# Moving the decode keys ahead of the attention, and the zero rows behind it, in a hybrid decoder step

## The chip, the core and the metric

The kernel runs as one program on one core of a Trainium2 chip. The metric is device microseconds (us) of one execution. The engines are named as in the profile: PE (TensorE), DVE (VectorE), ACT (ScalarE), POOL (GpSimd) and SP (SyncE), which here only issues DMAs. PEld is PE's loading of weights.

## The reference, cut to what matters

One layer is computed for 512 prompt tokens and for 8 sequences that each decode 4 tokens against a cache of 2048 rows.

```python
h = rmsnorm(x, norm1_g) * (1 + sc1) + sh1
z = h @ w_in                                  # columns q | k | v | u
att = dilated_attn_prompt(q, k, v, rel_bias)  # prompt: three dilated windows, 8 heads x 64
att = dilated_attn_decode(q, concat(past_k, k), concat(past_v, v), rel_bias)  # samples
ssm_y = s5_branch(u, h0, ...)                 # scan, GELU, per-group GLU
mixed = concat([rmsnorm(att), rmsnorm(ssm_y)])
x = x + g1 * (mixed @ w_out)
x = x + g2 * hier_moe(rmsnorm(x, norm2_g) * (1 + sc2) + sh2)
y = rmsnorm(x)
```

## The kernel before

The order of the work on each engine is written out by hand; engines meet through counting semaphores, and an engine that waits holds back all that follows on it. The stages that matter here follow each other on PE:

1. **Values' projection.** `z_two(8)` to `z_two(11)` project the values, one block of 128 columns each, with `v_t(c)` turning a block over into `vrow`, and the 16 pieces of the SSM branch's GLU (`glu_in(n)` on PE, `glu_gate(n)` on ACT, `glu_out(n)` on DVE) in between.
2. **Flips.** `flip(h)`, one per head, makes the relative bias tile of a head by a matmul with a flipped identity; ACT copies it out (`bias_out`). Four blocks of decode keys of group 0 (`dec_keys(0, q)`) stand between the flips. Then 16 transposes of the SSM output (semaphore `ssT`).
3. **Attention of the prompt.** 16 steps `st`, for four pairs of heads and four tiles of 128 queries each; a tile of index `qt` has `m = 128 (qt + 1)` keys. A step is a chain: `scores(st)` on PE, `row_max(st)` on DVE, the exponential on ACT (`softmax`), the inverse on DVE, the product on POOL, `probs_t(st)` on PE two steps later, copies on ACT and DVE, `pv(st)` on PE three steps later. After each fourth step ACT copies a pair out (`pair_out`), and the next pair's first `pv` waits for that.
4. **Decode attention.** It is done for two groups of four sequences. For a group: `dec_keys` in four blocks, `dec_softmax` (DVE) and `dec_exp` (ACT), `dec_probs_t` (8 transposes on PE), `dec_probs` (copies on ACT and DVE), `dec_values` in four blocks, `dec_out` (DVE). Before the change, group 0's softmax stands ahead of the attention, its `dec_probs_t` in step 1, group 1's keys in steps 2 to 5, group 0's values in steps 9 to 12, group 1's `dec_probs_t` in step 13 and its values in steps 14 to 17.
5. **Output projection** `wo(p, half)`, which starts when ACT has written the last pair's part of `mixT`, then routing and the mixture of experts, whose weights stream in.

The cache is loaded by SP in 16 **cache blocks** `kv(0)` to `kv(15)`, then the two halves of `w_out` as `kv(16)` and `kv(17)`. Blocks 0 to 3 are group 0's keys, 4 to 7 group 1's keys (1792 KB each), 8 to 11 group 0's values, 12 to 15 group 1's values (2048 KB each, but 1024 KB for 11 and 15). They share three slots of a ring; `kv(i)` for i from 7 waits until `kvu`, the count of blocks used by PE, is i - 2 (for i from 2 to 5, i - 1; block 6 waits for the last value projection). SP issues in order: one blocked issue holds the next ones back. Among the blocks SP also issues the load of `mod3P`, the modulation rows for the later stages:

```python
for i in range(1, N_KV + 2):
    kv(i)
    if i == 9:
        sp.wait_ge(s("glut"), 16)
        for b in range(2):
            sp.wait_ge(s_modst[b], 64)
        sp.dma_start(mod3P[...], mod_rows(3, 2)).then_inc(s("mod3"), 16)
```

`mod_rows` reads, for each of the 128 partitions, 24 pieces of 128 floats out of `mod_d`; 1536 KB in all. POOL clears and fills `glu2` (the GLU's block diagonal weights) and `qbd` (the decode queries, block diagonal), writes 10 tiles of zero rows to `y_d` (5120 KB), takes part in each attention step, and later stores the rows `h2` and gathers them. In the rows below, L2053 is `z_half`, L2170 `glu_in`, L2182 `flip`, L2195 and L2202 `dec_keys`, L2217 and L2224 `dec_values`, L2280 `scores`, L2303 `pv`, L1955 every transpose, L2364 `wo`, L819 every operation of ACT.

Of the kernel before, what the change touches and what calls it, by code (L numbers as in the profile page):

```python
# [19 lines left out]
P = 128  # L20
# [24 lines left out]
EXTRA = 10  # L45
# [157 lines left out]
KMZ, PADT, BPAD, GLUB, QBD = range(1, 6)  # L203
# [25 lines left out]
def _build(nc, I, O, ctx):  # L229
# [82 lines left out]
    dPT = at("dPT", [P, 8, P], TAB + 12288)  # L312
# [149 lines left out]
    def _(sp):  # L462
# [106 lines left out]
        for i in range(1, N_KV + 2):  # L569
            kv(i)  # L570
            if i == 9:
                sp.wait_ge(s("glut"), 16)
                for b in range(2):
                    sp.wait_ge(s_modst[b], 64)
                sp.dma_start(mod3P[:, :, :].rearrange("p v (c j n) -> p (v c) j n", c=2, j=4),
                             mod_rows(3, 2)).then_inc(s("mod3"), 16)
# [92 lines left out]
    def _(pool):  # L669
# [65 lines left out]
        turn_back(4)  # L735
        turn_back(5)
# [13 lines left out]
        pool.wait_ge(s("xp"), len(BATCH))  # L750
        o(pool.memset(glu2[:, :, :, :], 0.0))
# [8 lines left out]
        o(pool.memset(qbd[:, :, :, :], 0.0))  # L760
        pool.wait_ge(s("za"), 8)
        for h in range(HEADS):
            r = slice(64 * (h % 2), 64 * (h % 2) + 64)
            o(pool.tensor_copy(qbd[r, :, h // 2, TDEC * h:TDEC * (h + 1)],
                               qkT[r, h // 2, 0:NS].rearrange("p (n t) -> p n t", t=TDEC)))
        pool.sem_inc(s("pool_prep"), 1)
        pool.dma_start(y_d[NREG * P:NTILE * P, :], I["zero"].partition_broadcast(EXTRA * P)).then_inc(s("yzero"), 16)
# [7 lines left out]


# [38 lines left out]
    def _(act):  # L815
# [175 lines left out]

        z_two(8)
# [8 lines left out]
        for n in range(7, 10):  # L1001
            glu_gate(n)
        z_two(11)
        v_out(2)
        for n in range(10, 13):
            glu_gate(n)
        v_out(3)
        f(vrow[0:NS, QT, :], ps[0:NS, 5, :], ACT.Copy).then_inc(s("ve"), 1)
# [22 lines left out]

        def dec_exp(g):
            act.wait_ge(s("dSm"), g + 1)
            f(dP[:, :], dP[:, :], ACT.Exp, bias=dstat[:, 4:5], accum_out=dstat[:, 5:6]).then_inc(s("dP"), 1)

        def dec_probs(g):
            act.wait_ge(s("dPt"), g + 1)
            if g:
                act.wait_ge(s("dOp"), g)
            f(dPT[:, 4:7, :], ps[:, 6, 0:3 * P].rearrange("p (a b) -> p a b", a=3), ACT.Copy)  # L1040
            f(dPT[0:NS, 7, :], ps[0:NS, 6, 3 * P:4 * P], ACT.Copy).then_inc(s("dPTe"), 1)
# [34 lines left out]
        dec_exp(0)  # L1076
        for st in range(NST + 3):
            if 2 <= st < NST + 2:
                probs_first(st - 2)
            if st < NST:  # L1080
                softmax(st)
            if st >= 3 and (st - 3) % QT == QT - 1:
                pair_out((st - 3) // QT)
            if 2 <= st < 10:
                ssm_square(st - 2)
            if st == 1:
                dec_probs(0)
            if st == 6:
                dec_exp(1)
            if st == 13:  # L1090
                dec_probs(1)
# [181 lines left out]
    def _(dve):  # L1273
# [260 lines left out]
        for n in range(16):  # L1534
            glu_out(n)

# [24 lines left out]

        dec_softmax(0)
        for q in (1, 3):
            dve.wait_ge(s("ssT"), q + 1)
            ts_(mixT[:, 4 + q, 0:SEQ], ps[:, (2, 3, 4, 7)[q], :], gains[:, 8 + q:9 + q], None, ALU.mult).then_inc(s("ssTe"), 1)
# [42 lines left out]
        for st in range(NST + 3):  # L1608
            if 1 <= st <= NST:
                inverse(st - 1)  # L1610
            if 2 <= st < NST + 2:
                probs_second(st - 2)
            if st < NST:
                row_max(st)
            if st == 1:
                dec_probs(0)
            if st in (11, 15):
                add_squares((st - 7) // 4)
            if st == 6:
                dec_softmax(1)  # L1620
            if st == 13:
                dec_out(0)
                dec_probs(1)
# [323 lines left out]
    def _(pe):  # L1947
# [199 lines left out]
        def v_t(c):  # L2147
# [5 lines left out]
            if c < 4:  # L2153
# [3 lines left out]
                tr(ps[0:NS, 5, P * c:P * (c + 1)], vT[:, c % 2, 0:NS]).then_inc(s("v"), 1)  # L2157
# [16 lines left out]
        def flip(h):  # L2174
# [3 lines left out]
            if h == 1:  # L2178
                pe.wait_ge(s("ve"), NT)
# [4 lines left out]
        def dec_keys(g, q):  # L2184

            r = ring_wait(pe, ("kv", 4 * g + q))
            if q == 0:
                if g == 0:
                    pe.wait_ge(s("pool_prep"), QBD)
                    pe.wait_ge(s("ve"), NT)  # L2190
# [48 lines left out]
        for n in range(3):  # L2239
            glu_in(n)  # L2240
        z_two(9)
        v_t(0)
        for n in range(3, 7):
            glu_in(n)
        z_two(10)
        v_t(1)
        for n in range(7, 10):
            glu_in(n)
        z_two(11)
        v_t(2)  # L2250
        for n in range(10, 13):
            glu_in(n)
        v_t(3)
        for h in range(2):
            flip(h)
        for n in range(13, 16):
            glu_in(n)
        for h in range(2, HEADS):
            flip(h)
            if h % 2 == 0:  # L2260
                dec_keys(0, h // 2 - 1)
        dec_keys(0, 3)
# [52 lines left out]
        for st in range(NST + 3):  # L2315
# [8 lines left out]
            if st == 1:  # L2324
                dec_probs_t(0)
            if 2 <= st < 6:
                dec_keys(1, st - 2)
            if 9 <= st < 13:
                dec_values(0, st - 9)
            if st == 13:  # L2330
                dec_probs_t(1)
            if 14 <= st < 18:
                dec_values(1, st - 14)
# [343 lines left out]
```

## Time and profile before

| what | value |
|---|---|
| three runs | 829.48 us median (827.67, 829.48, 833.77) |
| profiled execution | 830.8 us, its span 828.6 us |
| mean granted PE clock | 0.906 of full speed |
| PE busy | 672.9 us, 81% of the span |
| DMA | 211.86 MB, mean 256 GB/s |
| values' projection | about 202 to 246 us of the span |
| flips, keys of group 0 | 246 to 271 us |
| attention | 271 to 354 us |
| output projection, routing | 354 to 478 us |
| experts and end | 478 to 829 us |

The stages are read off the timeline of PE. The span leaves 2.2 us of the execution's own time outside.

### The profile page before, as it was taken

The numbers are of one execution on the slowest core, as the hardware profiler recorded it, in microseconds if no ns is written. First come the engines' busy times: TensorE is split into PE (matmuls) and PEld (weight loads), VectorE is DVE, ScalarE is ACT, GpSimd is POOL, SyncE is SP. The second block draws the span as 40 slices with busy tenths as digits, with TensorE's granted clock in tenths as the row PEclk, the third lists the DMA queues.
The fourth block names the chain that finished last, engine by engine and source line by source line (L and its number), as shares of the span: only waits on it lengthen the run. The fifth ranks groups of instructions, "written<-read, shape, count | busy, mean of one in ns | idle before, by whom it ended". The sixth has DMA issues, their size and how long they took to land.

```text
span 828.6 us, 11931 instructions
## 1 busy us (share of the span) xinstructions
PE 672.9 (81%) x4846; PEld 391.4 (47%) x4846; DVE 289.5 (35%) x691; ACT 176.2 (21%) x362; POOL 126.4 (15%) x224
## 2 busy tenths in 40 slices
PE   4668999999998875999994289876899999979800
PEld 3568787888862441434554244323344444323300
DVE  4799747741110542416634611100010011100047
ACT  6010421222232563422111001100110101100033
POOL 2310007559100331200000100000000000000040
PEclk9789999999999987999985589989899999999955
DMA  8995166656858979884219268999998549999562
GB/s 293 379 271 195 57 244 219 206 182 189 206 112 317 365 171 306 335 311 157 78 36 323 94 203 300 339 391 409 396 363 298 209 130 389 396 399 400 215 240 108
DMA packets 93580, 211.86 MB, mean 256 GB/s; under 512 B 8700, under 2 KB 15372, under 8 KB 93237
## 3 DMA queue, kind: packets, MB, share of 16 engines
q1 hardware_dynamic: 82550, 182.48, 62.3%
q0 software_dynamic: 4976, 18.37, 7.6%
q10 hardware_dynamic: 6000, 10.25, 3.4%
q8 instruction: 39, 0.64, 0.3%
q14 instruction: 15, 0.12, 0.1%
HBM read 197.42 MB, written 18.91 MB: 261 GB/s over the span
## 4 chain that ended last, share of the span: by engine, by line
PE 64%; DMA 14%; SPq 9%; DVE 6%; ACT 3%; issue 2%; POOL 1%; ACTq 0%; POOLq 0%; DVEq 0%
PE ps L2458 15%; PE ps L2053 11%; PE ps L2498 9%; PE ps L2364 7%; SPq L644 6%; DMA whalf<-in_w_down 5%; PE ps L1955 4%; DMA ring<-in_cache_v 4%; PE ps L2023 3%; PE ps L1961 3%; SPq L503 2%; DMA ring<-in_ada_w 2%; PE ps L2195 2%; PE ps L2170 1%; DMA ada_half<-in_ada_w 1%
## 5 line engine op out<-in xcount | busy, mean ns | idle before, releaser
L2458 PE MATMUL ps<-whalf,xgT 128*128 128x512 f32 (+2 forms) x576 | 175.1, 624 | 15.7 <-DMA whalf<-in_w_up 11.4
L2458 PEld LDWEIGHTS ps<-whalf,xgT 128*128 128x128 f32 (+2 forms) x576 | 67.5, 159 | 115.6 <-issue 110.7
L2498 PE MATMUL ps<-whalf,aT 128*128 128x512 f32 (+2 forms) x288 | 87.6, 625 | 13.8 <-DMA whalf<-in_w_down 11.9
L2053 PE MATMUL ps<-hT,ring 128*128 128x272 f32 x384 | 91.4, 394 | 0.0
L2053 PEld LDWEIGHTS ps<-hT,ring 128*128 128x128 f32 x384 | 71.8, 190 | 15.2 <-issue 1.4
L2498 PEld LDWEIGHTS ps<-whalf,aT 128*128 128x128 f32 (+2 forms) x288 | 33.3, 159 | 61.1 <-issue 58.7
L2364 PE MATMUL ps<-ring,mixT 128*128 128x512 f32 x128 | 60.0, 627 | 1.9 <-ACT mixT L819 1.9
L789 POOL DMA_INDIRECT xg<-h_d,gidx x12 | 11.5, 954 | 244.1 <-PE ps L1955 210.8
L2023 PE MATMUL ps<-hT,ring 128*32 128x136 f32 x1024 | 36.4, 301 | 5.4 <-DVE hT L1355 4.0
L1842 DVE COPY ysb<-ps 128x512 f32<-128x512 f32 x12 | 8.3, 691 | 92.3 <-PE ps L2498 92.3
L2364 PEld LDWEIGHTS ps<-ring,mixT 128*128 128x128 f32 x128 | 25.2, 201 | 32.2 <-issue 30.0
L773 POOL TENSOR_TENSOR Sb<-Sb,stat 128x128 f32<-128x128 f32 (+3 forms) x32 | 22.3, 719 | 113.1 <-DVE stat L1593 113.1
L1829 DVE SCALAR_TENSOR_TENSOR a_s<-a_t,ps 128x512 f32<-128x512 f32 x12 | 8.3, 688 | 89.6 <-ACT a_t L819 89.6
L1835 DVE SCALAR_TENSOR_TENSOR a_s<-a_s,ps 128x512 f32<-128x512 f32 x12 | 8.2, 687 | 88.7 <-PE ps L2458 88.7
L2023 PEld LDWEIGHTS ps<-hT,ring 128*32 128x32 f32 x1024 | 34.4, 119 | 6.3 <-ACT hT L819 4.2
L819 ACT ACTIVATE ysb<-ps 128x512 f32<-128x512 f32 x12 | 7.2, 597 | 106.0 <-PE ps L2498 106.0
L819 ACT ACTIVATE a_t<-ps 128x512 f32<-128x512 f32 x12 | 7.2, 597 | 101.2 <-PE ps L2458 101.2
L819 ACT ACTIVATE xgT<-ps 128x512 f32<-128x512 f32 x12 | 7.2, 596 | 83.8 <-PE ps L1955 83.8
L809 POOL DMA_INDIRECT yg<-y_d,sidx x10 | 10.1, 1015 | 96.2 <-DMA y_d<-ysb 93.5
L2217 PE MATMUL ps<-ring,dPT 128*32 128x512 f32 x112 | 15.4, 665 | 8.5 <-DMA ring<-in_cache_v 8.5
L819 ACT ACTIVATE Sb<-Sb,stat 128x128 f32<-128x128 f32 (+3 forms) x32 | 17.7, 553 | 20.1 <-DVE stat L1587 20.1
L1961 PE MATMUL ps<-ada_half,silu_c 128*32 128x128 f32 x512 | 18.3, 275 | 4.0 <-issue 2.3
(396 smaller groups left out, 913.2 us busy)
## 6 DMA issues: line engine op xcount, KB each, us to landing
whalf<-in_w_down SPq DMA_DIRECT2D x32, 1024.0 KB, 16.1
whalf<-in_w_gate SPq DMA_DIRECT2D x32, 1024.0 KB, 10.2
whalf<-in_w_up SPq DMA_DIRECT2D x32, 1024.0 KB, 14.7
ada_half<-in_ada_w SPq DMA_DIRECT2D x16, 1024.0 KB, 5.4
ring<-in_cache_k SPq DMA_DIRECT2D x8, 1792.0 KB, 7.4
ring<-in_cache_v SPq DMA_DIRECT2D x6, 2048.0 KB, 13.1
ring<-in_ada_w SPq DMA_DIRECT2D x4, 2048.0 KB, 14.6
ring<-in_w_in SPq DMA_DIRECT2D x4, 2048.0 KB, 13.2
```

The costliest lines, as they stand in the source:

```text
L503: sp.dma_start(cq[n][:, :, 0, :], I[name]).then_inc(s("ctl"), 16)
L644: sp.dma_start(half_dst(w, i), half_src(w, expert[m], half)).then_inc(efull[i], 16)
L773: tt(Sb[:, b, n, 0:m], Sb[:, b, n, 0:m], stat[:, 36 + 2 * b + n:37 + 2 * b + n].broadcast_to([P, m]), ALU.mult).then_inc(s("pn"), 1)
L819: return nc.scalar.activation(out, in_, func, **kw)
L1955: return mm(out, lhsT=in_, rhs=ident[0:n, 0:n], start=True, stop=True, is_transpose=True)
L1961: ins = mm(out[32 * j:32 * j + 32, 0:P], cS[:, k, :], r[:, 512 * (k - k0) + P * j:512 * (k - k0) + P * (j + 1)], start=k == 0, stop=k == K ...
L2023: ins = mm(ps[32 * j:32 * j + 32, b % 2, NCOL * i:NCOL * (i + 1)], r[:, 512 * k + c0:512 * k + c0 + 32], hT[:, k, j, :], start=k == 0, sto ...
L2053: ins = mm(ps[:, z % 2, 0:2 * NCOL], r[:, 512 * k + P * (c % 4):512 * k + P * (c % 4 + 1)], hT[:, k, 2 * h:2 * h + 2, :].rearrange("p a b ...
L2195: ins = mm(ps[32 * n4:32 * n4 + 32, 5 + part, 0:c1 - c0], qbd[:, 4 * g + n4, q, :], r[:, CK * n4 + c0:CK * n4 + c1], start=q == 0, stop=q ...
L2364: ins = mm(ps[:, 2 * half + n, :], mixT[:, k, tok(j)], r[:, 512 * k:512 * (k + 1)], start=k % 4 == 0, stop=k % 4 == 3)
L2458: ins = mm(out[cols, :], xgT[b][:, k, cols], r[:, 512 * (k % 4):512 * (k % 4 + 1)], start=k == 0, stop=k == KD - 1, **tile_at(m_, n))
L2498: ins = mm(ps[cols, 6 + n2, :], aT[:, t % 2, c, cols], r[:, c0:c0 + 512], start=c == 0, stop=c == 3, **tile_at(m_, n))
```

## The change

Group 0's keys go among the values' projection, with their softmax, exponential, transposes and copies; group 1's keys go among the last GLU pieces and the flips, with softmax and exponential ahead of the attention. In the attention remain group 1's transposes (step 1), group 0's values (steps 3 to 6), group 1's copies (step 7) and group 1's values (steps 8 to 11). `dPT` gets another place, the samples' part of `vrow` another PSUM bank (7 for 5). On POOL, `glu2` is cleared before the last `turn_back`, `qbd` is filled before `glu2`, and the zero rows are written after the attention's products. On SP, `mod3P` is issued after block 14 instead of block 9.

```diff
-KMZ, PADT, BPAD, GLUB, QBD = range(1, 6)
+KMZ, PADT, BPAD, QBD, GLUB = range(1, 6)
-    dPT = at("dPT", [P, 8, P], TAB + 12288)
+    dPT = at("dPT", [P, 8, P], CQR + 16384)
         for i in range(1, N_KV + 2):
             kv(i)
-            if i == 9:
+            if i == 14:
                 sp.wait_ge(s("glut"), 16)
...
         turn_back(4)
+        pool.wait_ge(s("xp"), len(BATCH))
+        o(pool.memset(glu2[:, :, :, :], 0.0))
         turn_back(5)
...
-        pool.wait_ge(s("xp"), len(BATCH))
-        o(pool.memset(glu2[:, :, :, :], 0.0))
+        o(pool.memset(qbd[:, :, :, :], 0.0))
+        pool.wait_ge(s("za"), 8)
+        for h in range(HEADS):
+            r = slice(64 * (h % 2), 64 * (h % 2) + 64)
+            o(pool.tensor_copy(qbd[r, :, h // 2, TDEC * h:TDEC * (h + 1)],
+                               qkT[r, h // 2, 0:NS].rearrange("p (n t) -> p n t", t=TDEC)))
+        pool.sem_inc(s("pool_prep"), 1)
         pool.wait_ge(s("glul"), 32)
...
         pool.sem_inc(s("pool_prep"), 1)
-        o(pool.memset(qbd[:, :, :, :], 0.0))
...
-        pool.dma_start(y_d[NREG * P:NTILE * P, :], I["zero"].partition_broadcast(EXTRA * P)).then_inc(s("yzero"), 16)
         for st in range(HEADS // 2 * QT):
...
+        pool.dma_start(y_d[NREG * P:NTILE * P, :], I["zero"].partition_broadcast(EXTRA * P)).then_inc(s("yzero"), 16)
 @@ ACT, values' projection @@
         for n in range(7, 10):
             glu_gate(n)
+        dec_exp(0)
         z_two(11)
         v_out(2)
+        dec_probs(0)
         for n in range(10, 13):
             glu_gate(n)
 @@ ACT, attention @@
-        dec_exp(0)
+        dec_exp(1)
         for st in range(NST + 3):
...
-            if st == 1:
-                dec_probs(0)
-            if st == 6:
-                dec_exp(1)
-            if st == 13:
+            if st == 7:
                 dec_probs(1)
 @@ DVE @@
+        for n in range(10):
+            glu_out(n)
         dec_softmax(0)
+        dec_probs(0)
+        for n in range(10, 16):
+            glu_out(n)
+        dec_softmax(1)
...
-            if st == 1:
-                dec_probs(0)
-            if st == 6:
-                dec_softmax(1)
-            if st == 13:
+            if st == 7:
                 dec_out(0)
                 dec_probs(1)
 @@ PE, flip and dec_keys @@
             if h == 0:
                 pe.wait_ge(s("toep"), 16 * HEADS)
-            if h == 1:
                 pe.wait_ge(s("ve"), NT)
...
                 if g == 0:
                     pe.wait_ge(s("pool_prep"), QBD)
-                    pe.wait_ge(s("ve"), NT)
+                    pe.wait_ge(s("buread"), 6)
@@ PE, order @@
         for n in range(3):
             glu_in(n)
+        dec_keys(0, 0)
         z_two(9)
         v_t(0)
         for n in range(3, 7):
             glu_in(n)
+        dec_keys(0, 1)
         z_two(10)
         v_t(1)
         for n in range(7, 10):
             glu_in(n)
+        dec_keys(0, 2)
+        dec_keys(0, 3)
         z_two(11)
         v_t(2)
+        dec_probs_t(0)
         for n in range(10, 13):
             glu_in(n)
         v_t(3)
+        dec_keys(1, 0)
         for h in range(2):
             flip(h)
         for n in range(13, 16):
             glu_in(n)
+        dec_keys(1, 1)
         for h in range(2, HEADS):
             flip(h)
-            if h % 2 == 0:
-                dec_keys(0, h // 2 - 1)
-        dec_keys(0, 3)
+            if h in (3, 5):
+                dec_keys(1, h // 2 + 1)
 @@ PE, attention @@
             if st == 1:
-                dec_probs_t(0)
-            if 2 <= st < 6:
-                dec_keys(1, st - 2)
-            if 9 <= st < 13:
-                dec_values(0, st - 9)
-            if st == 13:
                 dec_probs_t(1)
-            if 14 <= st < 18:
-                dec_values(1, st - 14)
+            if 3 <= st < 7:
+                dec_values(0, st - 3)
+            if 8 <= st < 12:
+                dec_values(1, st - 8)
```

## Rows read from the trace of the kernel before

**Rows 1.** Chain that ended last, 195 to 360 us: start, length, what.
```profile
290.07 33.72 DMA ring<-in_cache_v
```
**Rows 2.** Timeline of PE before the attention: start, us, line, tiles, form, count [idle before].
```profile
252.41 1.71 PE L2195 MATMUL ps<-ring,qbd 128*32 128x512 f32 x16
...
261.21 1.71 PE L2195 MATMUL ps<-ring,qbd 128*32 128x512 f32 x16 [1.63 <-DMA ring<-in_cache_k]
...
265.92 3.19 PE L2195 MATMUL ps<-ring,qbd 128*32 128x512 f32 x16 [1.95 <-DMA ring<-in_cache_k]
268.86 0.68 PE L2202 MATMUL ps<-qkT,qbd 128*32 128x32 f32 x32
269.47 1.96 PE L1955 MATMUL ps<-const,ssm_tok 128*128 128x128 f32 x16
271.37 0.49 PE L2280 MATMUL ps<-qkT 64*128 64x128 f32 x4
```
**Rows 3.** Timeline of PE in the attention.
```profile
291.63 0.92 PE L2280 MATMUL ps<-qkT 64*128 64x384 f32 x4
295.81 0.44 PE L2303 MATMUL ps<-PTs,vrow 128*64 128x128 f32 x4 [3.26 <-ACT attT L819]
...
296.76 2.08 PE L2280 MATMUL ps<-qkT 64*128 64x512 f32 x4
...
305.84 1.92 PE L2217 MATMUL ps<-ring,dPT 128*32 128x512 f32 x16
...
314.22 1.13 PE L2280 MATMUL ps<-qkT 64*128 64x512 f32 x4
323.84 3.64 PE L2217 MATMUL ps<-ring,dPT 128*32 128x512 f32 x16 [8.49 <-DMA ring<-in_cache_v]
...
328.80 0.49 PE L2280 MATMUL ps<-qkT 64*128 64x128 f32 x4
329.23 1.07 PE L2217 MATMUL ps<-ring,dPT 128*32 128x512 f32 x8
...
333.68 1.09 PE L1955 MATMUL ps<-const,dP 128*128 128x128 f32 x8
...
351.20 1.09 PE L2303 MATMUL ps<-PTs,vrow 128*64 128x128 f32 x16
354.22 8.83 PE L2364 MATMUL ps<-ring,mixT 128*128 128x512 f32 x16 [1.93 <-ACT mixT L819]
```
**Rows 4.** Timeline of SP's queue, issues around `mod3P`: start, us of the issue.
```profile
285.97 0.37 SPq L561 DMA_DIRECT2D ring<-in_cache_v  x1
286.46 0.43 SPq L575 DMA_DIRECT2D mod3P<-mod_d  x1
...
290.07 16.01 SPq L561 DMA_DIRECT2D ring<-in_cache_v  x1
```
**Rows 5.** Windows: busy times of engines, granted clock, DMA share, GB/s.
```profile
294.00:296.00 2.00, 0.19 (x4) 0.23 (x4) 1.48 (x7) 1.97 (x6) 0.34 (x1) 1.00 1.14 360
296.00:298.00 2.00, 2.00 (x12) 0.93 (x9) 0.42 (x1) 2.00 (x3) 1.27 (x2) 0.68 0.53 82
298.00:300.00 2.00, 0.92 (x4) 0.08 (x4) 1.11 (x3) 1.87 (x5) 0.00 (x0) 0.50 0.38 80
...
312.00:314.00 2.00, 0.73 (x7) 0.59 (x8) 0.17 (x1) 1.97 (x5) 1.08 (x2) 1.00 0.78 55
...
318.00:320.00 2.00, 0.00 (x0) 0.00 (x0) 0.17 (x1) 0.47 (x2) 1.19 (x2) 0.50 1.01 410
```
**Rows 6.** DMA issues, 180 to 480 us: count, KB each, median us to landing.
```profile
ring<-in_cache_k SPq DMA_DIRECT2D x7, 1792.0 KB, 7.4
...
y_d<-in_zero POOLq DMA_DIRECT2D x1, 5120.0 KB, 29.0
```
**Rows 7.** Timeline of POOL: the clearing of `glu2`, the last step's product.
```profile
195.09 3.53 POOL L751 MEMSET glu_blocks<- 128x4096 f32 x1
...
345.81 2.04 POOL L773 TENSOR_TENSOR Sb<-Sb,stat 128x512 f32<-128x512 f32 x2 [4.28 <-DVE stat L1593]
```

More of the change, by code:

```diff
@@ L759, in _ @@
         pool.sem_inc(s("pool_prep"), 1)
-        o(pool.memset(qbd[:, :, :, :], 0.0))
[L761 to L766, printed above, removed]
-        pool.dma_start(y_d[NREG * P:NTILE * P, :], I["zero"].partition_broadcast(EXTRA * P)).then_inc(s("yzero"), 16)
         for st in range(HEADS // 2 * QT):
@@ L990, in bias_out, with dec_exp, dec_probs @@
             f(biasT[:, h, :], ps[:, (7, 4)[h % 2], :], ACT.Copy).then_inc(s("bfe"), 1)
+        def dec_exp(g):
+            act.wait_ge(s("dSm"), g + 1)
+            f(dP[:, :], dP[:, :], ACT.Exp, bias=dstat[:, 4:5], accum_out=dstat[:, 5:6]).then_inc(s("dP"), 1)
+        def dec_probs(g):
+            act.wait_ge(s("dPt"), g + 1)
+            if g:
+                act.wait_ge(s("dOp"), g)
+            f(dPT[:, 4:7, :], ps[:, 6, 0:3 * P].rearrange("p (a b) -> p a b", a=3), ACT.Copy)
+            f(dPT[0:NS, 7, :], ps[0:NS, 6, 3 * P:4 * P], ACT.Copy).then_inc(s("dPTe"), 1)
         z_two(8)
@@ L1007, in _ @@
         v_out(3)
-        f(vrow[0:NS, QT, :], ps[0:NS, 5, :], ACT.Copy).then_inc(s("ve"), 1)
+        f(vrow[0:NS, QT, :], ps[0:NS, 7, :], ACT.Copy).then_inc(s("ve"), 1)
         bias_out(0)
@@ L1030, in _ @@
             f(mixT[:, 4 + q, 0:SEQ], ps[:, (2, 3, 4, 7)[q], :], ACT.Copy, scale=gains[:, 8 + q:9 + q]).then_inc(s("ssTe"), 1)
[L1032 to L1041, printed above, removed]
         NST = HEADS // 2 * QT
@@ L1532, in glu_out @@
                 op0=ALU.add, op1=ALU.mult).then_inc(s("glug"), 1)
-        for n in range(16):
-            glu_out(n)
         def dec_softmax(g):
@@ L2156, in v_t @@
                     ins = tr(ps[:, 4, P * t:P * (t + 1)], vT[:, c % 2, NS + P * t:NS + P * (t + 1)])
-                tr(ps[0:NS, 5, P * c:P * (c + 1)], vT[:, c % 2, 0:NS]).then_inc(s("v"), 1)
+                tr(ps[0:NS, 7, P * c:P * (c + 1)], vT[:, c % 2, 0:NS]).then_inc(s("v"), 1)
         def glu_in(n):
```

## The prediction

> **What bounds the kernel now.** I read the chain that ended last first, then the timeline of PE through the stages of the change, then SP's issues, then the DMA traffic in windows. The longest single piece of the chain between 195 and 360 us is a cache load of 33.72 us [rows 1]. Up to the attention PE is the bound: the values' projection, GLU pieces and flips run end to end, except that two key blocks wait for their loads, 1.63 and 1.95 us, and the second then runs at half speed, 3.19 us for a block that takes 1.71 otherwise [rows 2]. In the attention the bound changes from step to step between PE and the softmax chain, until PE stands 8.49 us before group 0's third value block and then runs it in 3.64 us instead of 1.92 [rows 3]. The block it waits for, cache block 10, was issued at 290.07, long before its use, so the question is what it waited behind. SP's queue shows it: block 9 at 285.97, `mod3P` at 286.46, block 10 at 290.07, whose issue alone took 16.01 us [rows 4]. The windows show why: the DMA engines move 360 to 410 GB/s until about 295.5, then 55 to 82 GB/s until about 315, then 410 again [rows 5]. 1536 KB at some 80 GB/s is 20 us, so that valley is `mod3P`, and block 10 went through the same queue behind it. From block 9's issue to block 10's landing at 323.8 it is 37.9 us.
>
> So what the change does to keys, softmax and values has to be weighed together with a line that its title doesn't name: `mod3P` moves from ahead of block 10 to ahead of block 15.
>
> **Part by part.** The values' projection and flips (one sum for PE, which is the bound there). Added: four key blocks of group 1 at 1.64 from start to start, 6.6 us; their new keys, 0.45; group 0's eight transposes, 1.0. Removed: the waits 1.63 and 1.95 and the 1.5 us of half speed, 5.1 us [rows 2]. The waits go because loads start earlier: block 0's use moves from 252.4 to about 212 (behind three GLU pieces), so block 2 is issued near 214 and used near 237, block 3 near 227 and 239, block 4 near 239 and 254, block 5 near 241 and 261, block 6 near 249 and 265, block 7 near 256 and 269. The least of these distances is 12 us, where a key block lands after 7.4 us [rows 6]. New on the path: ACT's two copies of group 0's probabilities stand ahead of GLU gate 10, about 0.6, and the last flip's copy on ACT, about 0.7, was hidden by the last key block and is not any more. The wait of `flip(0)` for all of `vrow` lies behind key block 4, which hides it; without that cover it costs 0.3. Sum 8.1 - 5.1 + 1.3 - 0.3 = **+3.9**, bounds +2.5 (neither of the new waits) and +5.2 (GLU pieces delayed twice as much). The first scores move from 271.4 to 275.3. DVE's and ACT's softmax of both groups lies beside projections and flips and costs nothing there; if PE were not the bound it would be about 3 us a group.
>
> POOL. Clearing `glu2` is 3.53 us [rows 7]; it goes into a wait of POOL ahead of the last `turn_back`, and as `qbd`'s part is pulled ahead of the copies into `glu2` by about as much, `glu2` is ready near 208, as before, where PE wants it at 209. I count 0; at worst 3.5 us of delay of the scan's last output, which PE would see.
>
> Attention, steps 0 to 11. Steps 2 to 5 lose key blocks and steps 3 to 6 get value blocks of 1.9 us [rows 3]; ACT and DVE lose group 1's exponential and softmax in step 6, and get both halves of the copies in step 7. Following scores, maximum, exponential, product, transposes and copies with the durations of the same steps before, the scores of step 6 come 1.2 us earlier against the first ones (three value blocks of 1.9 for four key blocks of 1.64), those of step 8 2.9 us (PE's wait for the first pair's copy is 1.3 instead of 3.26), and those of step 11 only 0.2 us, since step 8 held no decode work before and now has a value block, 1.9, and 1.3 of waiting for the copies. **-0.2**, bounds -2 and +1.
>
> The stall. Block 14 may be issued when group 0's last value block is used (`kvu` 12), in step 6, about 1.9 us after its scores. `mod3P` follows at once, and block 15, for which step 8 gives leave, stands behind it. Before, from scores 6 (291.63) to scores 11 (314.22) 22.6 us passed [rows 3]; with three value blocks in between instead of two and the copies of step 7 I take 23.5, so PE reaches group 1's last block 23.5 - 1.9 + 1.1 = 22.7 us after `kvu` 12. Block 15 lands later than that: the queue still holds part of block 13 and all of block 14, about 9.4 us at 400 GB/s, as much as it held ahead of `mod3P` before, so of the 37.9 us above only the half size of block 15 goes off, 2.6 us, and about 35.2 remain. PE stands 35.2 - 22.7 = 12.5 us, at 319 to 331.6, against 8.5 us before: **+4.0**. Bounds: with only block 14 ahead 10 us, with a slower end of `mod3P` 14 us. The loads of block 10, 11 and 12 to 14 are ahead of `mod3P` and each lands 5 us or more before its use. What runs right behind the stall is at half speed again, about 3.7 us, as before (3.64): 0.
>
> Steps after the stall. Between scores 12 (328.80) and the start of the output projection (354.22) three PE groups stood on the path: the end of group 0's values (2.0, from 329.23), group 1's transposes (1.0, from 333.68) and, at the end, values ahead of the last `pv` (351.20) [rows 3]. The last step's product on POOL ended at 347.85 [rows 7]; transposes and copy take 1.25 us from there, so that `pv` could have begun at 349.1, 2.1 us earlier. Of the 5.1 us I count **-4.7**, because the row maximum then ends last in step 12 and 13; bounds -3.5 and -5.1.
>
> PE's clock in the last steps. Before, PE idled 3.26 us for a pair's copy at 292.5 to 295.8 after a busy stretch, and the granted clock then fell to 0.68 and 0.50, scores of 512 taking 2.08 us instead of 1.13 [rows 3, 5]. After the change step 14 has no value block, and the chain there (maximum, exponential, copy of the pair) leaves PE idle for the same 3.26 us between scores 14 and `pv(12)`. Then scores 15 (+1.0), half of the last transposes (+0.4) and the last `pv` (+1.0) run at half speed: **+2.4**, or 0 if the clock holds. I take 2.4, as the row is the nearest one there is. The output projection began at half clock before too (8.83 us for a block of about 7.1), so nothing changes there.
>
> Zero rows. They are 5120 KB and took 29.0 us to land [rows 6]. Now they are issued near 354, beside the first expert halves, rows of x and the samples' modulation. The bound is the chain of PE, ACT and DVE there, and what it needs next from memory, the third tile's rows of x and the storing of the first tile's `h2` rows (which POOL issues behind the zero rows), is due near 410. All traffic due by then is about 50 us of the DMA engines from 351 on: 0, with some 10 us to spare. It is no gain either, since nothing waited for DMA when the zero rows were written before, except that it slows no cache load now.
>
> Sum: 3.9 - 0.2 + 4.0 - 4.7 + 2.4 = **+5.4 us**. The profiled execution took 830.8 us (span 828.6 and 2.2 around it), so it would take 836.2; the median of the runs is 1.3 us lower, and there the forecast is 829.48 + 5.4 = 834.9, rounded 835. All that follows, the experts' stream above all, starts later by the same and is not changed by it. With the bounds, most of them not at once, this case by itself lies between 829 and 839.
>
> The Trainium skill speaks against the stall: the page "DMA: Bandwidth & Descriptors", section "Specifications", gives 512 B as the smallest transfer at line rate, and pieces of 128 floats are just that. By its 358 GB/s `mod3P` would take an estimated 4.4 us, and block 15 would land ahead of its use. The trace disagrees: 55 to 82 GB/s while `mod3P` has the queue alone [rows 5]. I go by the row.
>
> **The rivals.** First, a clear queue: `mod3P` doesn't hold block 15 for as long as PE needs to reach it, because it is faster beside other traffic or because the blocks ahead are done sooner. Then scores 12 follow at about 322.4 instead of 328.8, 6.4 us earlier, and with the gain of 4.7 behind and the clock's 2.4 or 0 it is -8.7 to -11.1 us: 818 to 821. For it speaks that all blocks up to 14 are early; against it the same `mod3P` in [rows 4, 5], which held a block for 18 us with nothing else in the queue. 0.10. In between, a stall of 3 to 7 us gives 822 to 828: 0.08.
>
> Second, slower: the zero rows overrun. Its place is the third tile of the output projection: POOL's store of the first `h2` tile, if served in order behind the zero rows, lets ACT overwrite that buffer only near 402, and SP's rows of x for the third tile share the engines with the zero rows. It decides from the point where either lands after about 410; from there each us is paid in full. A write at half the rate (58 us for 29) would put it at 412 to 420, so +2 to +10 on top: 841 or so. Against it: the prefetches share evenly and none of them is due before 478. 0.08.
>
> Third, the change doesn't do what it says, since keys of group 0 wait for their loads in the projection as they did in the flips: 3.6 us more in that stage, but the stall behind it is counted from step 6 and comes later by the same. It would be 838 to 839; at 12 us distance I give it no chance of its own.
>
> **How the numbers follow.** Forecast 0.74 (829 to 839 and a little beyond), clear queue 0.10, short stall 0.08, zero rows 0.08. The range leaves out the clear queue and the far end of the zero rows and reaches a little beyond the forecast's own bounds: 824 to 842. A measurement of this kernel tells about 1%, 8.3 us, from no change: faster means below 821.2, slower above 837.8. The clear queue is faster, mostly; the zero rows and the upper end of the forecast, with a tenth of it, are slower: 0.09, 0.75, 0.16.
>
> **What would show it.** Right: no wait of PE for key blocks; first scores near 275; `mod3P` issued near 297 with a slow issue of block 15 behind it; a wait of PE of 10 to 14 us for cache values, now at the last block of group 1 and in step 11; some 21 to 23 us from scores 12 to the output projection, part of it at clock 0.5. Wrong: no such wait, with the output projection before 346; or a wait of ACT or DVE for rows of x or `h2` between 390 and 430; or a GLU piece that waits for POOL at 209.

## The result, and the profile after

The changed kernel takes 839.12 us (median of 4 runs, 836.52 to 842.36), the kernel before beside it 828.94 us (4 runs, 827.67 to 833.77). The ratio is 1.0097, 95% interval 1.0056 to 1.0137, which is 4.6 to 11.4 us more (the two medians alone stand at 1.0123, 10.2 us). The forecast was +5.4 us, 835.0. The profiled execution of after, the fastest of its four runs, took 836.5 us (span 834.2), that of before 830.8 (span 828.6): +5.7.

The stages in front of the change differ by a microsecond or more from one profiled execution to the next. So times in the attention are counted here from one event, the first product of the GLU. In the timeline of PE it stands, in the kernel before, at

```profile
209.03 3.09 PE L2170 MATMUL ps<-glu_blocks,u_chunks 128*128 128x256 f32 x12
```

and in the kernel after, with the rows that answer to [rows 2, 3]:

```profile
210.40 3.09 PE L2167 MATMUL ps<-glu_blocks,u_chunks 128*128 128x256 f32 x12
...
255.33 1.71 PE L2191 MATMUL ps<-ring,qbd 128*32 128x512 f32 x16
...
275.51 0.49 PE L2282 MATMUL ps<-qkT 64*128 64x128 f32 x4
...
305.94 3.49 PE L2213 MATMUL ps<-ring,dPT 128*32 128x512 f32 x16 [1.99 <-ACT dPT L819]
...
320.28 1.13 PE L2282 MATMUL ps<-qkT 64*128 64x512 f32 x4
331.07 1.94 PE L2213 MATMUL ps<-ring,dPT 128*32 128x512 f32 x8 [9.66 <-DMA ring<-in_cache_v]
...
337.32 0.80 PE L2282 MATMUL ps<-qkT 64*128 64x128 f32 x4
...
347.45 0.69 PE L2305 MATMUL ps<-PTs,vrow 128*64 128x128 f32 x4 [3.26 <-ACT attT L819]
...
349.12 2.08 PE L2282 MATMUL ps<-qkT 64*128 64x512 f32 x4
```

No key block has a wait any more. The first scores are at 275.51 (forecast 275.3). The one wait for a cache load has moved to group 1's last value block, behind scores 11, and ends at 331.07 (forecast 331.6). Both times are counted from the span's start and hold 1.4 us that this execution lost ahead of the first GLU product, outside the change. Later PE stands 3.26 us for a pair's copy, and then come scores of 512 at 2.08 us instead of 1.13. Three pieces of the chain that ended last (start, length, what) answer to [rows 1]:

```profile
309.47 21.55 DMA ring<-in_cache_v
...
331.07 1.94 PE ps L2213 x8
...
361.30 8.55 PE ps L2362 x16
```

SP's issues answer to [rows 4]. `mod3P` is issued at 296.80, as forecast (297). The slowest issue is not, as forecast, that of the cache block behind it (4.58 us) but that of `w_out` behind the block (12.35 us for its two halves):

```profile
296.80 0.48 SPq L575 DMA_DIRECT2D mod3P<-mod_d  x1
309.47 4.58 SPq L561 DMA_DIRECT2D ring<-in_cache_v  x1
314.10 12.35 SPq L554 DMA_DIRECT2D ring<-in_w_out  x2
```

The windows answer to [rows 5]; the last two columns are DMA share and GB/s, the one before them the granted clock:

```profile
298.00:300.00 2.00, 1.48 (x10) 1.09 (x12) 0.43 (x2) 1.97 (x3) 1.61 (x2) 0.83 1.00 393
...
312.00:314.00 2.00, 2.00 (x20) 0.56 (x22) 0.97 (x6) 0.96 (x4) 0.00 (x0) 1.00 0.56 86
...
322.00:324.00 2.00, 0.00 (x0) 0.00 (x0) 1.53 (x6) 0.99 (x3) 0.00 (x0) 0.81 0.63 59
328.00:330.00 2.00, 0.00 (x0) 0.00 (x0) 0.00 (x0) 0.00 (x0) 0.00 (x0) 0.50 1.05 409
348.00:350.00 2.00, 2.00 (x8) 1.22 (x8) 0.42 (x1) 1.84 (x3) 0.71 (x1) 0.50 0.05 12
```

The valley is the same as before, only later: 393 GB/s at 298 to 300, and so on up to 306, 52 to 92 in the windows from 308 to 326, while `mod3P` is under way, and 409 when the last block comes. Of the DMA issues, two answer to [rows 6]; nobody waited for either of them behind the attention:

```profile
y_d<-in_zero POOLq DMA_DIRECT2D x1, 5120.0 KB, 32.1
...
mod3P<-mod_d SPq DMA_DIRECT2D x1, 1536.0 KB, 31.5
```

From the first GLU product to four later events of the PE timelines (scores 0, 11, 12 and the output projection), in us, from one profiled execution of each kernel, and the times of all runs; each ratio is to the kernel before on the same chip:

| kernel | scores 0 | scores 11 | scores 12 | output proj. | median us | ratio, 95% interval |
|---|---|---|---|---|---|---|
| before | 62.3 | 105.2 | 119.8 | 145.2 | 828.94 | 1 |
| after | 65.1 | 109.9 | 126.9 | 150.9 | 839.12 | 1.0097 (1.0056 to 1.0137) |
| e1_mod3p_last | 65.2 | 109.9 | 114.3 | 137.5 | 829.16 | 0.9913 (0.9877 to 0.9949) |
| e2_old_order_mod3p_last | 60.6 | 103.5 | 107.8 | 133.2 | 822.09 | 0.9859 (0.9804 to 0.9913) |
| e3_mod3p_after_9 | 65.1 | 123.4 | 127.9 | 153.1 | 842.18 | 1.0112 (1.0080 to 1.0143) |
| e4_zero_rows_early | 74.1 | 116.2 | 137.5 | 161.4 | 849.15 | 1.0145 (1.0087 to 1.0203) |
| e5_values_late | 65.1 | 108.7 | 114.8 | 140.4 | 828.84 | 0.9932 (0.9898 to 0.9967) |
| e6_mod3p_on_act | 65.2 | 110.1 | 129.0 | 152.4 | 838.55 | 1.0090 (1.0057 to 1.0123) |
| e7_wide_pieces_probe | 65.1 | 108.7 | 113.2 | 136.4 | 820.65, one run | |
| e8_narrow_pieces_probe | 65.1 | 110.0 | 114.4 | 138.9 | 828.86, one run | |
| e9_old_order_two_keys_early | 59.0 | 101.8 | 106.1 | 131.6 | 821.15 | 0.9856 (0.9813 to 0.9898) |
| e10_new_order_mod3p_wide | 65.0 | 107.7 | 112.2 | 136.8 | 825.24 | 0.9898 (0.9851 to 0.9945) |
| e11_two_keys_early_mod3p_wide | 59.0 | 101.8 | 106.1 | 131.5 | 819.86 | 0.9832 (0.9791 to 0.9873) |
| e12_old_order_mod3p_wide | 61.0 | 103.9 | 108.2 | 133.7 | 822.94 | 0.9882 (0.9838 to 0.9926) |

The kernel before stood at 833.1 us (833.04 to 833.14) beside all the experiments, so their medians are read by the ratio and not against 828.94.

### The profile page after: what moved, and what is told of

It is laid out like the page before. It is cut to its first block, busy times and chain, and to the rows that moved or that the text cites. A ratio compares the mean times of both kernels' runs of the same rounds, so it can differ in the third digit from the quotient of the medians.

```text
span 834.2 us, 11931 instructions
## 1 busy us (share of the span) xinstructions
PE 673.4 (81%) x4846; PEld 390.1 (47%) x4846; DVE 289.7 (35%) x691; ACT 176.7 (21%) x362; POOL 126.5 (15%) x224
## 4 chain that ended last, share of the span: by engine, by line
PE 64%; DMA 12%; SPq 10%; DVE 7%; ACT 3%; issue 3%; POOL 1%; ACTq 0%; POOLq 0%; DVEq 0%
PE ps L2456 15%; PE ps L2050 11%; PE ps L2496 9%; PE ps L2362 7%; SPq L644 6%; DMA whalf<-in_w_down 5%; PE ps L1952 4%; PE ps L2020 3%; DMA ring<-in_cache_v 3%; PE ps L1958 2%; SPq L503 2%; DMA ring<-in_ada_w 2%; PE ps L2191 2%; PE ps L2167 1%; PE ps L2213 1%
## 5 line engine op out<-in xcount | busy, mean ns | idle before, releaser
L2362 PE MATMUL ps<-ring,mixT 128*128 128x512 f32 x128 | 57.8, 608 | 1.9 <-ACT mixT L819 1.9
L772 POOL TENSOR_TENSOR Sb<-Sb,stat 128x128 f32<-128x128 f32 (+3 forms) x32 | 22.3, 718 | 125.6 <-DVE stat L1594 125.6
## 6 DMA issues: line engine op xcount, KB each, us to landing
ring<-in_cache_v SPq DMA_DIRECT2D x6, 2048.0 KB, 10.5
```

Of the source, the lines that this page charges most:

```text
L772: tt(Sb[:, b, n, 0:m], Sb[:, b, n, 0:m], stat[:, 36 + 2 * b + n:37 + 2 * b + n].broadcast_to([P, m]), ALU.mult).then_inc(s("pn"), 1)
L2362: ins = mm(ps[:, 2 * half + n, :], mixT[:, k, tok(j)], r[:, 512 * k:512 * (k + 1)], start=k % 4 == 0, stop=k % 4 == 3)
```

## The experiments

**Is the stall `mod3P`'s?** e1 leaves the changed order as it is and issues `mod3P` behind the last load of the list; e2 does the same in the kernel before; e3 puts it back to its old place in the new order.

```diff
 e1 (after):   -            if i == 14:    +            if i == N_KV + 1:
 e2 (before):  -            if i == 9:     +            if i == N_KV + 1:
 e3 (after):   -            if i == 14:    +            if i == 9:
```

> The changed kernel with the load of mod3P issued behind the second half of w_out instead of behind cache block 14. Queue theory (block 15 waits in SP's queue behind mod3P): PE has no wait for cache values left, the scores of step 12 come 11 to 12 us earlier (the wait of 9.7 and the half clock behind it), the output projection starts near 348 instead of 361, and mod3P, which then lands near 345, is in time for its first use; 826 to 828 us if the changed kernel is 839. Bandwidth theory (the caches as a whole come too late, whatever their order): a wait of 5 us or more for cache values stays, the time is 834 or more. Late-mod3P rival: DVE waits for mod3P at its first product in the output projection, and the time falls by less than 6 us.

> The kernel before, with nothing changed but mod3P, issued behind the second half of w_out instead of behind cache block 9. Queue theory: PE's wait of 8.5 us for cache block 10 and the half clock behind it go (about -10 us in the attention), but here w_out is issued only in the attention's last steps, near 337, so mod3P lands near 366 and DVE, which wants it near 365, may wait 0 to 5 us: -5 to -10 us, 819 to 824. If moving the decode keys is what matters and not mod3P: within 3 us of the kernel before, with the wait for cache blocks moved to a later one.

> The changed kernel with mod3P issued behind cache block 9, where it was before. Queue theory: the next block behind it pays: mod3P is issued near 268, the queue is clear of it near 296 to 299, block 10 lands near 301 to 304 and is wanted near 291, so PE waits about 10 to 12 us for cache values in step 5 and not in step 11; time within 4 us of the changed kernel's. Place theory (the title's move of keys and values is what costs, mod3P's new place is what made it slower): the wait is 3 us or less, and the time is at or below that of the kernel before.

In e1 no wait of PE for a cache load is left, and the output projection starts 13.4 us earlier than in after (137.5 against 150.9). In e2 the wait for block 10 is gone and the two for keys stay (1.62 and 1.84 us). In e3 the stall goes to the block that follows `mod3P` there, in step 5, as the timeline of PE shows:

```profile
308.19 3.64 PE L2213 MATMUL ps<-ring,dPT 128*32 128x512 f32 x16 [13.60 <-DMA ring<-in_cache_v]
```

So the stall follows `mod3P` through the list, in both orders. e1 against e2 shows a second thing: with the same `mod3P` the new order reaches the output projection 4.3 us later than the old one in these traces. The times point the same way: the intervals of the two ratios overlap, but on the one chip where both ran the mean of e1's 11 runs is 827.4 us and that of e2's 5 is 822.8.

**Do the zero rows matter?** e4 writes them where they were, ahead of the attention's products, and leaves the rest of after.

```diff
+        pool.dma_start(y_d[NREG * P:NTILE * P, :], I["zero"]...)   (ahead of the products)
...
-        pool.dma_start(y_d[NREG * P:NTILE * P, :], I["zero"]...)   (behind them)
```

> The changed kernel with the zero rows written where they were before, ahead of the attention's products on POOL. Theory of the prediction (they are hidden in either place): within 3 us of the changed kernel; the loads of key blocks 2 and 3 take longer, 10 to 14 us, but land before their use. Rival (the zero rows at their new place hold back the output projection): 3 to 6 us less than the changed kernel, gained between 361 and 485 of its span. Other rival: key blocks 2 or 3 come too late, PE waits for them, and it is slower.

PE waits for a key block, and the block behind the wait runs at half speed, 3.21 us for 1.71:

```profile
252.48 3.21 PE L2192 MATMUL ps<-ring,qbd 128*32 128x512 f32 x16 [7.32 <-DMA ring<-in_cache_k]
```

The first scores are 9.0 us later than in after and the stall behind scores 11 grows to 13.86 us. So the theory that the zero rows are hidden in either place is wrong: with the keys taken early, the zero rows have to move.

**Is it also the time at which the block is used?** e5 leaves `mod3P` where after has it and uses group 1's values three steps later.

```diff
-            if 8 <= st < 12:
-                dec_values(1, st - 8)
+            if 11 <= st < 15:
+                dec_values(1, st - 11)
```

> The changed kernel with group 1's values in steps 11 to 14 instead of 8 to 11; mod3P stays behind block 14. Queue theory (block 15 lands some 35 us after group 0's last value block, whenever it is wanted): it is wanted three steps, about 12 us, later than in the changed kernel, so PE's wait for cache values falls from 10 to 14 us to 3 us or less, the output projection starts 8 to 12 us earlier, and the time is 8 to 12 us below the changed kernel's. Also PE has work in the last steps again, so that its clock should hold there. Rival (the wait is for the caches as a whole, or moves along with the use): PE waits 8 us or more in step 14 and the time stays within 4 us of the changed kernel's.

No wait for the caches is left, and the output projection starts at 140.4, 10.5 us before after's. Part of the tail's gain is given back: scores 12 to output projection take 25.6 us, against 23.2 in e1.

**Is it the order in SP's queue?** e6 takes `mod3P` off SP and lets ACT issue it on a queue of its own at the end of step 6.

```diff
-            if i == 14:
-                ...
-                sp.dma_start(mod3P..., mod_rows(3, 2))
...
+            if st == 6:
+                ...
+                act.dma_start(mod3P..., mod_rows(3, 2))
```

> The changed kernel with mod3P issued by ACT at the end of step 6, on ACT's own queue, at nearly the same moment as SP issued it. If order within SP's queue is what holds block 15 back: block 15 is loaded beside mod3P, PE's wait falls to 3 us or less, and the time is 9 to 13 us below the changed kernel's, near that of mod3P last. If it is mod3P's work on the DMA engines that all share, whatever the queue: block 15 still lands 8 us or more late, and the time stays within 4 us of the changed kernel's.

The timelines of e6, in order of time: ACT's issue of `mod3P`, SP's of block 15 and of `w_out`, and the wait of PE:

```profile
299.98 0.38 ACTq L1086 DMA_DIRECT2D mod3P<-mod_d  x1
...
310.51 0.37 SPq L561 DMA_DIRECT2D ring<-in_cache_v  x1
315.38 14.64 SPq L554 DMA_DIRECT2D ring<-in_w_out  x2
...
334.40 1.93 PE L2213 MATMUL ps<-ring,dPT 128*32 128x512 f32 x8 [11.49 <-DMA ring<-in_cache_v]
```

Windows of e6, while `mod3P` is under way and behind it:

```profile
312.00:314.00 2.00, 2.00 (x20) 1.18 (x22) 1.13 (x4) 0.60 (x1) 0.00 (x0) 1.00 0.55 88
...
324.00:326.00 2.00, 0.00 (x0) 0.00 (x0) 1.03 (x4) 1.50 (x4) 0.00 (x0) 0.80 0.42 48
...
332.00:334.00 2.00, 0.00 (x0) 0.00 (x0) 0.00 (x0) 0.00 (x0) 0.00 (x0) 0.50 1.04 398
```

Block 15 is issued in 0.37 us with nothing slow ahead of it on SP's queue, and still lands 23.8 us later. The core moves 48 to 114 GB/s from 310 to 328, all queues together, and 301 to 402 from 328 to 340. The packets by queue say more. From 314 to 320, all that moves is ACT's queue (q10); SP's (q1), on which block 15 was issued at 310.51, moves nothing. The last row, from the window 310 to 314, has block 15 with its time from issue to landing:

```profile
DMA packets 874, 0.45 MB, mean 75 GB/s; under 512 B 0, under 2 KB 874, under 8 KB 874
q10 hardware_dynamic: 874, 0.45, 53.7%
...
ring<-in_cache_v SPq DMA_DIRECT2D x1, 1024.0 KB, 23.8
```

So the wait doesn't need the order within SP's queue: a load on another queue is held as well.

**What makes `mod3P` slow?** It reads 24 pieces of 512 B, 16 KB apart, the same 24 for each of the 128 partitions. Two probes add a load of the same 1536 KB behind block 14, into the same tile, and issue the real `mod3P` last; what the added load brings is overwritten. e7 reads one piece of 12 KB, the same for all partitions; e8 reads 24 pieces of 512 B, 2 KB apart, other ones for each partition.

```diff
 e7: + bass.AP(mod_d.tensor, 4 * P * P, [[0, P], [1, 3 * D]])
 e8: + bass.AP(I["w_in"].tensor, 0, [[8 * 2 * D, P], [2 * D, 6], [4 * P, 4], [1, P]])
```

> mod3P itself is issued last; behind cache block 14, where the change has it, stands a load of the same 1536 KB into the same place, read from the same table in one piece of 12 KB for each partition instead of 24 pieces of 512 B, all partitions from the same addresses; the real load overwrites it. If the small pieces make mod3P slow: it takes 4 to 6 us, block 15 is in time, no wait of PE for cache values. If it is slow because 128 partitions read the same few rows: 15 us or more, and PE waits 8 to 14 us for block 15 as in the changed kernel.

> As the probe with wide pieces, but the load behind block 14 reads 24 pieces of 512 B for each partition from addresses that no other partition reads (out of w_in); mod3P itself is issued last. If the small pieces make such a load slow whatever they hold: 50 to 95 GB/s for 15 to 20 us, and PE waits 8 to 14 us for block 15. If it takes both (small pieces and the same addresses): 4 to 8 us, no wait.

A window of e7 with the added load under way:

```profile
306.00:308.00 2.00, 0.17 (x4) 0.16 (x8) 1.81 (x8) 2.00 (x7) 1.08 (x2) 1.00 1.08 436
```

Windows of e8, with the added load and then with the real `mod3P`:

```profile
312.00:314.00 2.00, 2.00 (x26) 1.59 (x22) 0.00 (x0) 0.43 (x1) 0.00 (x0) 1.00 1.19 289
...
334.00:336.00 2.00, 0.00 (x0) 0.00 (x0) 0.69 (x5) 1.24 (x5) 0.50 (x1) 0.98 0.95 89
```

Neither added load is slow, and neither makes PE wait. Shortness alone is not the cause (e8), and neither is reading the same bytes for all partitions (e7); short pieces together with repeated addresses are slow. e8 differs from `mod3P` in the distance between pieces too, 2 KB for 16 KB, and in the table that it reads, so repetition, distance and table are not told apart.

**Is there a better version?** e9 keeps the kernel before but issues `mod3P` last and takes two key blocks within the projection, two behind flips 3 and 5, with the waits and the PSUM bank of `vrow` changed as this needs. e10 to e12 first gather the 24 pieces into one row of 12 KB in DRAM, by ACT, and read that row for all partitions: e10 in the order of after, e11 in that of e9, e12 in that of before, with `mod3P` in the old place of each order (behind block 14 in e10, behind block 9 in e11 and e12).

```diff
 e9:  +        dec_keys(0, 0)   ...   +        dec_keys(0, 1)      (in the projection)
      +            if h in (3, 5):
      +                dec_keys(0, h // 2 + 1)
 e10 to e12:
+        act.dma_start(mod_c.rearrange("(a j n) -> a j n", a=6, j=4),
+                      bass.AP(mod_d.tensor, 4 * P * P, [[P * P, 6], [32 * P, 4], [1, P]]))
...
-                sp.dma_start(mod3P..., mod_rows(3, 2))
+                sp.dma_start(mod3P..., bass.AP(mod_c.tensor, 0, [[0, P], [1, 3 * D]]))
```

> The order of the kernel before with mod3P last (as in the second run) and only key blocks 0 and 1 moved among the values' projection, blocks 2 and 3 between the flips, group 1's keys, all values and the zero rows where they were. Theory that PE's waits for key blocks 2 and 3 are all that the early keys can save: these two waits (1.6 and 1.8 us) go, first scores 3 to 4 us earlier after the first GLU piece than with mod3P last alone (57 instead of 60.6), 3 us below it in time, a ratio to the kernel before of about 0.982. Rival (the blocks cost PE as much among the projection as their waits cost, or the zero rows delay block 2): within 1.5 us of it, 0.986.

> The changed kernel, mod3P behind block 14 as there, but the 24 rows are first gathered into one row of 12 KB in memory by a small copy that ACT issues after GLU gate 2, and mod3P reads that row, one piece for each partition. If piece size is the whole cost of mod3P's place: it takes 4 to 6 us, no wait of PE for cache values, output projection 136 to 138 us after the first GLU piece, ratio to the kernel before 0.985 to 0.992. If the wait has another part: 3 us or more of it stay and the ratio is above 0.995.

> The old order with key blocks 0 and 1 among the projection, and mod3P as one piece for each partition, behind block 9. Expected from the sum of the parts: no wait of PE for caches, none of DVE for mod3P (1.8 us before its place last), output projection 129 to 132 us after the first GLU piece, ratio 0.980 to 0.985. Rival: block 10 still lands late, 3 to 5 us of wait, ratio 0.987 or more.

> The kernel before with nothing changed but mod3P's read, one piece for each partition, in its old place behind block 9. If piece size is what made PE wait for block 10: no wait for cache values, output projection 132 to 134 us after the first GLU piece, ratio 0.982 to 0.987. If order of issue and not the length of the transfer counts: a wait of 5 us or more for block 10 stays.

e9 loses both waits for keys and has its first scores 1.7 us earlier than e2, less than the 3 to 4 us expected, and its time can't be told from e2's (0.9856 and 0.9859). The last place of `mod3P` has a price of its own in the old order: DVE waits for it at its first product behind the output projection, 3.44 us in e2 and 4.47 in e9, as the timeline of DVE shows for e9:

```profile
368.24 1.28 DVE L1664 SCALAR_TENSOR_TENSOR pt<-ps,rssm,pt 128x1024 f32<-128x1024 f32 x1 [4.47 <-DMA mod3P<-mod_d]
```

How much of that the total pays is not shown; e1, e11 and e12 have no such wait. In e10 to e12 `mod3P` stays early and PE has no wait for it; the DMA issues of e11 show it landing in less than half the time (14.7 us from its issue, with the cache block ahead of it counted in, for 31.5 in after):

```profile
mod3P<-mod_c SPq DMA_DIRECT2D x1, 1536.0 KB, 14.7
```

e11 has the lowest ratio, 0.9832 (0.9791 to 0.9873), and is faster than both kernels, by 1.3 to 2.1% than the kernel before. Its interval overlaps those of e2, e9, e10 and e12. e10 and e12, the two orders with the wide read, can't be told apart by time either (0.9898 and 0.9882); in their traces the new order reaches the output projection 3.1 us later.

## Why the prediction was right, and where its steps were off

The forecast held in sign and in place: the kernel got slower, and group 1's last value block waits for `mod3P`. e1, e3 and e5 show `mod3P` as the cause of that wait: with the load moved behind the block, or the block used later, the wait is gone, and with `mod3P` elsewhere in the list it stands elsewhere. The wait alone is not why the change costs time, since the kernel before has one of 8.49 us too: without it on either side (e1 and e2) the new order still reaches the output projection 4.3 us later. The forecast's +5.4 us lies in the interval of +4.6 to +11.4, near its lower end; the median is 4.1 us above the forecast, and where these 4 us come from is not shown.

**Projection and flips**, +3.9 (the terms as written add up to 4.0), measured +2.8 (65.1 - 62.3), within its bounds. The waits and the half speed of [rows 2] are gone, as counted. Of the two new waits one is there, 0.78 us for ACT's copy of the last flip; behind GLU gate 10 the timeline shows none. The half speed, however, is not a lasting part of the old order. In e2 both waits for keys are there, but the block behind the second runs at full speed:

```profile
269.61 1.71 PE L2195 MATMUL ps<-ring,qbd 128*32 128x512 f32 x16 [1.84 <-DMA ring<-in_cache_k]
```

Its first scores are at 60.6 (61.0 in e12), and `mod3P`, issued behind the first scores in the kernel before too, has no part in that. Against e2 the new order costs 4.6 us there.

**Steps 0 to 11**, -0.2, measured +1.9 (109.9 - 65.1 = 44.8 against 42.9), outside its bound of +1. Up to scores 8 the forecast fits (2.9 us earlier, measured 3.1), so the miss lies in step 8. There the value block waits 1.99 us for ACT's copies, where I counted 1.3, and then runs at half clock, 3.49 us for 1.92, which I did not count. That half clock comes and goes between executions of the same order: the block takes 3.33 us in e1 and 3.62 in e8, but 1.92 in e7 and e10, where steps 0 to 11 take 43.6 and 42.7 us, e10's as forecast.

**The stall**, +4.0 by 12.5 against 8.5 us. From `mod3P`'s issue to the block it is 331.07 - 296.80 = 34.3 us; by the same reckoning the forecast is 34.8 (37.4 before, from 286.46 to 323.84, less 2.6). PE, however, comes to the block 24.6 us after that issue (34.3 - 9.66) instead of 22.3 (34.8 - 12.5), through the step above, and so the wait is shorter in this execution. Where the same wait was seen again it was 11.49 (e6) and 13.86 (e4). From scores 11 to scores 12 it is 17.0 us for 14.6; of these +2.4 the wait gives 1.2 (9.66 for 8.49). The rest is half clock behind the wait, for which I counted nothing beyond what was there before: the granted clock stays at 0.50 up to 340, 9 us from the block's start, where in the kernel before it was back at 1.00 from 328 on, 4 us from it. Up to scores 12 the three terms give 3.9 - 0.2 + 4.0 = 7.7; measured 126.9 - 119.8 = 7.1.

**Behind the stall**, -4.7 + 2.4 = -2.3, measured -1.4 (24.0 against 25.4); 24.0 lies above the 21 to 23 us that were named as a sign. The clock is as forecast: granted 0.50 in 348 to 350 behind an idle 3.26 us, scores 15 at 2.08 us. Up to the output projection the sum is +5.7 measured, +5.4 forecast, although its terms are off by 0.9 to 2.1 us, in both directions: that the sums lie so close is luck. What follows takes 474.4 us before and 472.9 after, and the head ahead of the first GLU product 1.4 us more: 5.7 - 1.5 + 1.4 = 5.6, the difference of the two spans.

**The mechanism was wrong in one detail**: "block 10 went through the same queue behind it". The block's place behind `mod3P` in one queue is not needed for the wait; e6 gives `mod3P` another queue and the block waits as long. While `mod3P` runs in e6, all queues together move 48 to 114 GB/s. What limits that, and what holds the other queue back, is not shown: the DMA engines stand at a busy share of 0.42 to 0.64 in those windows.

The page "DMA: Bandwidth & Descriptors" of the Trainium skill, section "Queues, rings and completion order", says that each DMA engine takes turns between the queues it has work for, packet by packet. By that the block in e6 would come through beside `mod3P`; the trace disagrees, with 23.8 us from issue to landing for 1024 KB and 874 packets on one queue against none on the other from 314 to 320. (Whether the block's packets stood ready at the engines by then, the trace doesn't show.) The section "Specifications" of the same page of the Trainium skill, which the prediction weighed, has 512 B as enough for line rate. e8 comes near that (289 to 331 GB/s in the windows from 308 to 314, where the cache blocks ahead of it moved at 397 to 420), `mod3P` with the same 512 B does not (48 to 99 GB/s in the traces of before, after and e6 to e8, once the blocks ahead of it are through; the kernel before reaches 99 in the window from 300 to 302, where the prediction read 55 to 82): the size of a piece does not decide alone.

**Zero rows**, 0: right for the change as made, since no wait appears behind the attention. "It is no gain either" was wrong. e4 puts 7.32 us of wait on a key block and 9.0 us on the first scores. The sentence that every key block has 12 us of distance held only because the zero rows had gone; I had taken them off without a price. The third rival, with no chance of its own, is what e4 shows.

**The clear queue**, 818 to 821, is what e1 makes of after: 0.9913, some 7.2 us (4.2 to 10.2) below the kernel before, where 8.7 to 11.1 were reckoned. Without its stall the new order would look like a success; e2 and e12 show that the gain is the removed `mod3P` wait (0.9859 and 0.9882 without any of the new order), and that the new order adds nothing to it. By the traces of e1 and e2 it costs +4.6 to the first scores, +1.8 in steps 0 to 11 (mostly the half clock of step 8), +0.1 up to scores 12 and -2.2 behind them, 4.3 us in all; by those of e10 and e12 +4.0, -0.2, +0.1 and -0.9, 3.1 us.

## What to carry to other kernels

Before moving work to an earlier place, list what else is issued among the loads that it needs, and price those by what a trace shows of loads with the same source pattern, not by their bytes. Here a broadcast from scattered short rows was cheaper gathered first into one contiguous row (e12, 0.9882 of the kernel before). And when a forecast's sum comes out right, check its terms one by one: here errors of +2.1 and -1.5 us (steps 0 to 11, and scores 11 to 12) hid one another. And look at a second trace of the same order before counting a half-speed block as a gain or a cost.

## What the runs showed of the hardware that was not expected

The same 1536 KB into the same tile were slow or fast by their source alone: 24 pieces of 512 B, repeated for 128 partitions, at 48 to 99 GB/s; 24 such pieces, each partition its own, at 289 to 331; one piece of 12 KB for all partitions at 436. While the first was under way, a load on another queue did not come through either: from 314 to 320 its queue moved no packet, the slow load's 874 (e6).

The stretch from the output projection to the gathered rows, in which PE's work is the same in all these kernels, takes 120 to 122 us in some profiled executions and 124 to 128 in others, and each of the two orders is found among both. One place where the two part is a tile of router products and the output projection's products behind it. The timeline of PE has there in the kernel before

```profile
412.49 3.36 PE L2390 MATMUL ps<-rw,h2T 128*128 128x20 f32 x16
415.69 15.92 PE L2364 MATMUL ps<-ring,mixT 128*128 128x512 f32 x32
```

and in the kernel after

```profile
419.29 1.96 PE L2388 MATMUL ps<-rw,h2T 128*128 128x20 f32 x16
421.10 13.98 PE L2362 MATMUL ps<-ring,mixT 128*128 128x512 f32 x32
```

The same products take 3.36 and 15.92 us in the one and 1.96 and 13.98 in the other; the granted clock is 0.50 from 414 to 418 in the one, and 1.00 throughout in the other. Differences of 3 to 6 us arise there which the change has no part in, as large as most of what was measured here, so that the events up to the output projection say more on the change than the total.
